# A fused encoder layer on one core: x and the small vectors laid out channel by channel, and the first two weight tiles taken slice by slice

## The chip, the cores and the metric

The kernel runs on one core of a Trainium2 chip. The metric is the device time of one execution in microseconds (us), as the median of several runs. A profiled execution of the same program gives the trace from which all rows below are taken.

## What is computed

One encoder layer on 256 tokens (a grid of 4 rows by 64 columns) with 2048 channels, all in float32. The part that matters here is the beginning:

```python
xn = rmsnorm(x, norm_pre_w)        # x (1, 256, 2048); scale by rsqrt(mean(x*x) + 1e-6), times norm_pre_w
h  = xn @ w_in                     # w_in (2048, 13312)
na_q, na_k, na_v, na_z, hg_q, hg_ff, hg_fb, hg_i, hg_z, gate_pre = split(h)
# o_a: neighbourhood attention on na_*, 16 heads of 64; o_b: gated two-way recurrence on hg_*, 8 heads of 128
g_a, g_b = split(sigmoid(gate_pre + b_gate))
y   = g_a * (o_a @ w_branch[:1024]) + g_b * (o_b @ w_branch[1024:])
out = x + rmsnorm(y @ w_out, norm_post_w)
```

## The kernel before

All products are made of rounded halves. A float32 operand is split into a high part (rounded to the matmul's format, ScalarE) and a low part (the remainder, VectorE), and a product is hi*hi + lo*hi + hi*lo, three matmuls. Weights come in tiles of 1 MiB into `raw`, a ring of four slots that SP's queue fills (`load`, line 318); a tile is split in two halves, by `split_hi` on ScalarE (line 463) and `split_lo` on VectorE (line 721), into `w_hi` and `w_lo`, four halves each.

The program has a beginning of 16 weight tiles (`early_tile`, line 1244), then 8 groups of ten tiles and 8 gate tiles (`project`, line 1174), then the branch and output products. The beginning is four blocks of 512 output columns (values of the attention, then inputs of the recurrence); a block is four tiles, and tile r of a block covers contraction slices k = 4r to 4r + 3. A slice is 128 channels. Each slice of an early tile is six matmuls of 128 x 512: three parts times two halves of the tokens.

Within the beginning, x has to be turned: it lies token by token in memory and the products want channels on partitions. x is loaded in token rows by six transfers on SP's queue (`load_x`, line 352), which lie between the weight slices of the first two tiles (`first_weights`, line 362). TensorE transposes each 128 x 128 square into PSUM (`turn_x`, line 1205); ScalarE reads the square out as the high part, times `norm_pre_w` (`first_hi`, `x_hi`, lines 564 and 570), VectorE makes the low part (`first_lo`, `x_lo`, lines 996 and 1005). The factor of the norm that belongs to a token is applied later. It comes from squares of x (`square`, line 575, ScalarE), a power on GpSimd (line 425) and a scaled identity (`make_turner`, line 1017), from which TensorE makes a row of factors for channel-major use (line 1255, ahead of the second half of tile 5). `take_block` (line 584) uses it for the blocks' results, `scale_pair`, `act_hi` and `act_lo` (lines 1024, 594 and 1034) for x itself, one pair of slices to a tile.

The small vectors (bounds, gate biases, two norm weights) are loaded as rows by four transfers on ScalarE's queue and are transposed on TensorE too (lines 1399 and 1403).

What sets the order is each engine's own program, written out by hand, with semaphores between them. Lines 366 to 383 are SP's order at the start: x and weight slices 0 to 7 by turns, then a wait for slices 4 to 7 (line 378), tile 2, a wait for the last x (line 381), tiles 3 to 15. TensorE warms up with six products of ones (line 1396), waits for the identity, transposes the norm weight, and goes through `first_tile` (line 1228). ScalarE squares x between the splits of tiles 1 and 2 and behind the last slice of x (lines 620 and 627).

Of the kernel before, what the change touches and what calls it, by code (L numbers as in the profile page):

```python
# [32 lines left out]
P = 128  # L33
T = 256
# [29 lines left out]
WARM_UP = 6  # L64
KEEP_WARM = 2
FIRST_K = 4
# [33 lines left out]
def encoder_layer(nc, x, norm_pre_w, w_in, b_gate, band_bias, hg_lb_logits, hg_norm_w, w_branch,  # L100
                  w_out, norm_post_w, out):
# [4 lines left out]
    with ExitStack() as ctx:  # L106
# [17 lines left out]
        o_tok = big[:, 16:32, :].rearrange("p (t a) c -> p t (a c)", t=2)  # L124
        bias = sb("bias", [P, 2, 2 * BAND])
# [19 lines left out]
        first_rows = bias[:, :, :].rearrange("p a k -> p (a k)")  # L145
        vec_rows, norm_rows = first_rows[0:72, 0:P], first_rows[0:KT, P:2 * P]
        vec = sb("vec", [P, 88])
# [24 lines left out]
        def dec_of(level):  # L172
# [7 lines left out]
        turn_bank = (None, *bank[1:4], bank[7], bank[0], bank[6], bank[1])  # L180
        first_turned = (bank[0], bank[6])
        ps_norm, ps_vec = bank[4][:, 0:KT], bank[7][:, 0:72]
# [9 lines left out]
        first_landed = [sem(f"first_landed{k}") for k in range(2 * FIRST_K)]  # L192
# [8 lines left out]
        vec_landed, norm_landed, norm_turned, norm_ready = (  # L201
            sem("vec_landed"), sem("norm_landed"), sem("norm_turned"), sem("norm_ready"))
        x_landed = [[sem(f"x_landed{side}{t}") for t in range(2)] for side in range(2)]
        x_first_landed = [sem(f"x_first_landed{t}") for t in range(2)]
# [3 lines left out]
        vec_turned, vec_ready = sem("vec_turned"), sem("vec_ready")  # L208
# [3 lines left out]
        xt_done, xhi_ready, xn_ready = sem("xt_done"), sem("xhi_ready"), sem("xn_ready")  # L212
# [33 lines left out]
        def grid_rows(ap, t):  # L246

            return ap[0].rearrange("(r u c) d -> u c r d", r=ROWS, u=2)[t]
# [68 lines left out]
        def _(sp):  # L317
# [34 lines left out]
            def load_x(first_k, last_k, t, landed):  # L352
                cols = slice(first_k * P, last_k * P)
                sp.dma_start(x_tok[:, t, cols], grid_rows(x, t)[:, :, cols]).then_inc(landed, 16)
# [14 lines left out]
            for k in range(2, FIRST_K):  # L369
                first_weights(k)  # L370
# [1127 lines left out]
```

## Time and profile before

| | us |
|---|---|
| median of 3 runs | 815.03 (813.36 to 815.8) |
| profiled execution | 813.89 |
| its span on the core | 812.2 |
| TensorE busy (matmuls) | 800.6 (99%) |
| VectorE busy | 626.2 (77%) |
| ScalarE busy | 391.2 (48%) |
| GpSimd busy | 25.4 (3%) |
| mean granted TensorE clock | 0.998 |

The page gives busy time as a share of the span. Matmuls are pipelined, so one of 128 x 512 lasts 0.39 us in the trace while the next starts 0.23 us after it; a busy TensorE is to be read by starts, not by durations. The trace has 13919 instructions, 5672 of them matmuls, and 153.52 MB of transfers.

### The profile page before, as it was taken

The numbers are of one execution on the slowest core, as the hardware profiler recorded it, in microseconds if no ns is written. First come the engines' busy times: TensorE is split into PE (matmuls) and PEld (weight loads), VectorE is DVE, ScalarE is ACT, GpSimd is POOL, SyncE is SP. The second block draws the span as 40 slices with busy tenths as digits, with TensorE's granted clock in tenths as the row PEclk, the third lists the DMA queues.
The fourth block names the chain that finished last, engine by engine and source line by source line (L and its number), as shares of the span: only waits on it lengthen the run. The fifth ranks groups of instructions, "written<-read, shape, count | busy, mean of one in ns | idle before, by whom it ended". The sixth has DMA issues, their size and how long they took to land.

```text
span 812.2 us, 13919 instructions
## 1 busy us (share of the span) xinstructions
PE 800.6 (99%) x5672; PEld 692.9 (85%) x5672; DVE 626.2 (77%) x1079; ACT 391.2 (48%) x668; POOL 25.4 (3%) x45
## 2 busy tenths in 40 slices
PE   9999999999999999999999999999999999999995
PEld 7788888888888888888888888888888888888884
DVE  4777647888888889889889889889874887865543
ACT  5755435445445444444544444445445555444442
POOL 4000000000000000000000000000000000000002
PEclk9999999999999999999999999999999999999999
DMA  8856578676676676666766756657667776586522
GB/s 306 307 172 212 155 193 229 172 203 172 164 207 166 174 198 165 187 184 170 195 171 182 193 161 195 185 157 197 167 168 197 209 203 178 187 297 219 187 73 104
DMA packets 238528, 153.52 MB, mean 189 GB/s; under 512 B 3752, under 2 KB 219904, under 8 KB 238080
## 3 DMA queue, kind: packets, MB, share of 16 engines
q1 hardware_dynamic: 237456, 148.65, 63.6%
q10 hardware_dynamic: 1008, 3.98, 1.3%
q8 instruction: 45, 0.74, 0.4%
q14 instruction: 19, 0.16, 0.1%
HBM read 149.47 MB, written 2.10 MB: 187 GB/s over the span
## 4 chain that ended last, share of the span: by engine, by line
PE 94%; DMA 1%; ACT 1%; SPq 1%; DVE 1%; POOL 0%; issue 0%; POOLq 0%; ACTq 0%
PE psum L1186 47%; PE psum L1194 25%; PE psum L1441 3%; PE psum L1443 3%; PE psum L1442 3%; PE psum L1270 3%; PE psum L1272 3%; PE psum L1271 3%; DMA raw<-in_w_in 1%; PE psum L1313 1%; PE psum L1347 1%; PE psum L1299 1%; PE psum L1336 1%; PE psum L1286 0%; SPq L363 0%
## 5 line engine op out<-in xcount | busy, mean ns | idle before, releaser
L725 DVE TENSOR_TENSOR w_lo<-raw,w_hi 128x1024 fp32r<-128x1024 f32 x270 | 320.2, 1221 | 70.6 <-ACT w_hi L471 70.5
L1186 PE MATMUL psum<-act_hl,w_hi 128*128 128x512 f32 x1408 | 335.8, 391 | 0.0
L471 ACT ACTIVATE w_hi<-raw 128x1024 fp32r<-128x1024 f32 x270 | 272.7, 1054 | 64.0 <-PE psum L1272 34.0
L1186 PEld LDWEIGHTS psum<-act_hl,w_hi 128*128 128x128 f32 x1408 | 258.8, 188 | 50.1
L1194 PE MATMUL psum<-act_hl,w_lo 128*128 128x256 f32 x1408 | 185.5, 285 | 0.0
L1194 PEld LDWEIGHTS psum<-act_hl,w_lo 128*128 128x128 f32 x1408 | 178.1, 191 | 4.8
L485 ACT ACTIVATE part<-psum 128x256 f32<-128x256 f32 x88 | 33.6, 382 | 227.2 <-PE psum L1194 227.2
L1186 PE MATMUL psum<-branch_hl,w_hi 128*128 128x512 f32 x256 | 61.4, 391 | 0.7 <-DVE branch_hl L925 0.7
L1186 PEld LDWEIGHTS psum<-branch_hl,w_hi 128*128 128x128 f32 x256 | 47.0, 188 | 10.2 <-issue 1.1
L1441 PE MATMUL psum<-w_hi,act_hl 128*128 128x512 f32 x128 | 49.9, 390 | 0.3 <-DVE w_lo L725 0.3
L1443 PE MATMUL psum<-w_hi,act_hl 128*128 128x512 f32 x128 | 49.8, 389 | 0.0
L1442 PE MATMUL psum<-w_lo,act_hl 128*128 128x512 f32 x128 | 49.8, 389 | 0.0
L1270 PE MATMUL psum<-w_hi,branch_hl 128*128 128x512 f32 x120 | 47.2, 393 | 0.9 <-DVE w_lo L725 0.6
L1272 PE MATMUL psum<-w_hi,branch_hl 128*128 128x512 f32 x120 | 46.7, 389 | 0.0
L1271 PE MATMUL psum<-w_lo,branch_hl 128*128 128x512 f32 x120 | 46.7, 389 | 0.0
L1194 PEld LDWEIGHTS psum<-branch_hl,w_lo 128*128 128x128 f32 x256 | 32.8, 191 | 1.2
L1194 PE MATMUL psum<-branch_hl,w_lo 128*128 128x256 f32 x256 | 33.2, 283 | 0.0
L742 DVE TENSOR_TENSOR hg<-psum,part 128x256 f32<-128x256 f32 x32 | 18.2, 568 | 16.4 <-ACT part L485 15.7
L783 DVE STREAM_TRANSPOSE prob_t<-wide 32x128 f32<-32x128 f32 (+1 forms) x96 | 27.9, 291 | 1.5
L1441 PEld LDWEIGHTS psum<-w_hi,act_hl 128*128 128x128 f32 x128 | 24.0, 188 | 5.6 <-DVE w_lo L725 0.8
L1443 PEld LDWEIGHTS psum<-w_hi,act_hl 128*128 128x128 f32 x128 | 24.0, 188 | 5.1
L1442 PEld LDWEIGHTS psum<-w_lo,act_hl 128*128 128x128 f32 x128 | 24.0, 188 | 5.0
(136 smaller groups left out, 616.7 us busy)
## 6 DMA issues: line engine op xcount, KB each, us to landing
raw<-in_w_in SPq DMA_DIRECT2D x102, 1024.0 KB, 5.8
raw<-in_w_branch SPq DMA_DIRECT2D x16, 1024.0 KB, 5.9
raw<-in_w_out SPq DMA_DIRECT2D x16, 1024.0 KB, 5.1
raw<-in_w_in SPq DMA_DIRECT2D x8, 256.0 KB, 5.6
big<-in_x ACTq DMA_DIRECT2D x2, 1024.0 KB, 6.4
bias<-in_band_bias SPq DMA_DIRECT2D x8, 192.0 KB, 5.9
out<-big SPq DMA_DIRECT2D x5, 256.0 KB, 2.6
big<-in_x SPq DMA_DIRECT2D x4, 256.0 KB, 4.9
```

The costliest lines, as they stand in the source:

```text
L471: nc.scalar.activation(w_hi[:, (2 * r + h) % HALVES, :], raw[:, r, 1024 * h:1024 * (h + 1)], ACT.Copy).then_inc(hi_ready, 1)
L485: nc.scalar.activation(part[:, b, :], ps_proj[b][:, T:2 * T], ACT.Copy).then_inc(part_ready, 1)
L725: nc.vector.tensor_tensor(w_lo[:, i, :], raw[:, r, 1024 * h:1024 * (h + 1)], w_hi[:, i, :].bitcast(F32), ALU.subtract).then_inc(lo_ready, 1)
L783: ins = nc.vector.transpose(*turned_square(r, j))
L1186: nc.tensor.matmul(sums[h][:, :], w_hi[:, i, w], operand[:, k, :], start=k == 0 if whole else k % 8 == 0, stop=False, skip_group_check=True)
L1194: ins = nc.tensor.matmul(sums[h][:, 0:T], w_lo[:, i, w], operand[:, k, 0:T], start=False, stop=k == KT - 1 if whole else k % 8 == 7, skip_ ...
L1270: nc.tensor.matmul(sums, hi, w_hi[:, i, w], start=(k == 0), stop=False)
L1271: nc.tensor.matmul(sums, hi, w_lo[:, i, w], start=False, stop=False)
L1272: ins = nc.tensor.matmul(sums, lo, w_hi[:, i, w], start=False, stop=(k == KT - 1))
L1441: nc.tensor.matmul(o, hi, w_hi[:, i, w], start=(k == 0), stop=False)
L1442: nc.tensor.matmul(o, hi, w_lo[:, i, w], start=False, stop=False)
L1443: ins = nc.tensor.matmul(o, lo, w_hi[:, i, w], start=False, stop=(k == KT - 1))
```

## The change

On the host, x is given twice: `x_turned`, channel by channel (128 partitions, 16 slices, 256 tokens), and `x_rows`, token by token in the kernel's own order of tokens; the vectors come as one array of 128 partitions by 88. The output is written in the kernel's order of tokens and is put back on the host.

In the kernel, transposes of x and of the vectors are gone, with the matmuls that kept TensorE warm between them. x is loaded in pairs of slices, the first pair and the vectors on ScalarE's queue, the others on SP's, between the weight slices; weight tiles 0 and 1 go slice by slice, slices 0 to 7, through `first_split_hi`, `first_split_lo` and `first_products`, and slice 0's high part is made by VectorE. SP waits for no landing at the start. Token-major x, needed for the squares, is loaded behind tiles 4 and 5; squares, power, scaled identity, gate constants, `take_block(0)` and the scaling of x move one or two tiles later. The warm-up has nine products.

The core of the diff:

```diff
-WARM_UP = 6
-KEEP_WARM = 2
-FIRST_K = 4
+WARM_UP = 9
+FIRST_K = 8
...
+        x_cols = big[:, 16:32, :]
...
         def store(engine, t, c):
-            engine.dma_start(grid_rows(out, t)[:, :, c * 512:(c + 1) * 512],
+            engine.dma_start(out[t * P:(t + 1) * P, c * 512:(c + 1) * 512],
...
# SP
+            def load_cols(i):
+                sp.dma_start(x_cols[:, 2 * i:2 * i + 2, :], x_turned[:, 2 * i:2 * i + 2, :]).then_inc(cols_landed[i], 16)
...
-            for t in range(2):
-                load_x(0, FIRST_K, t, x_first_landed[t])
-                first_weights(t)
-            for k in range(2, FIRST_K):
-                first_weights(k)
-            for t in range(2):
-                load_x(FIRST_K, 8, t, x_landed[0][t])
-            for k in range(FIRST_K, 2 * FIRST_K):
-                first_weights(k)
-            for t in range(2):
-                load_x(8, KT, t, x_landed[1][t])
-            for k in range(FIRST_K, 2 * FIRST_K):
-                sp.wait_ge(first_landed[k], 16)
-            early(2)
-            for t in range(2):
-                sp.wait_ge(x_landed[1][t], 16)
-            for n in range(3, N_PRE):
-                early(n)
+            for i in range(FIRST_K // 2):
+                if i:
+                    load_cols(i)
+                for k in (2 * i, 2 * i + 1):
+                    first_weights(k)
+            for n in range(2, 4):
+                for i in (2 * n, 2 * n + 1):
+                    load_cols(i)
+                early(n)
+            for n in range(4, N_PRE):
+                early(n)
+                if n < 6:
+                    t = n - 4
+                    sp.dma_start(x_tok[:, t, :], x_rows[t * P:(t + 1) * P, :]).then_inc(rows_landed[t], 16)
...
# ScalarE
             def x_hi(k):
-                act.wait_ge(xt_done, k // 2 + 2)
-                nc.scalar.activation(x_hl[:, k, 0:T], turn_bank[k // 2][:, (k % 2) * T:(k % 2 + 1) * T], ACT.Copy,
+                if k % 2 == 0:
+                    act.wait_ge(cols_landed[k // 2], 16)
+                nc.scalar.activation(x_hl[:, k, 0:T], x_cols[:, k, :], ACT.Copy,
                                      scale=norm_w[:, k:k + 1]).then_inc(xhi_ready, 1)
+            def square(t):
+                wait(act, ss_ready, 2 * t)
+                act.wait_ge(rows_landed[t], 16)
+                for side in range(2):
+                    nc.scalar.activation(squares[side], x_tok[:, t, side * (D // 2):(side + 1) * (D // 2)], ACT.Square,
                                          accum_out=ssq[:, 2 * side + t:2 * side + t + 1]).then_inc(ss_ready, 1)
...
+            act.dma_start(x_cols[:, 0:2, :], x_turned[:, 0:2, :]).then_inc(cols_landed[0], 16)
+            act.dma_start(vec[:, :], vectors).then_inc(vec_landed, 16)
+            act.wait_ge(const_step, 1)
+            nc.scalar.activation(small[:, 124:125], ones[:, 0:1], ACT.Copy)
+            act.wait_ge(vec_landed, 16)
+            for k in range(FIRST_K):
                 x_hi(k)
+                if k > 0:
+                    first_split_hi(k)
+            for n in range(2, 4):
+                for h in range(2):
+                    x_hi(4 * n + 2 * h)
+                    x_hi(4 * n + 2 * h + 1)
+                    split_hi(*early_place(n), h)
+            for n in range(3, N_PRE):
                 split_tile(*early_place(n + 1))
-                if n % 4 == 0:
+                if 4 <= n < 6:
+                    square(n - 4)
+                if n == 6:
+                    take_block(0)
+                elif n % 4 == 0 and n > 4:
                     take_block(n // 4 - 1)
...
-                if 7 <= n < 15:
-                    act_hi(n - 7)
+                if 8 <= n < 16:
+                    act_hi(n - 8)
...
# VectorE
+            dve.wait_ge(first_landed[0], 16)
+            nc.vector.tensor_copy(w_hi[:, 0, 0:512], raw[:, 0, 0:512]).then_inc(first_copied, 1)
+            dve.wait_ge(vec_landed, 16)
+            for i in range(KT // 2):
+                dve.wait_ge(cols_landed[i], 16)
+                if i < FIRST_K // 2:
+                    for k in (2 * i, 2 * i + 1):
+                        x_lo(k)
+                        first_split_lo(k)
+                else:
+                    x_lo(2 * i)
+                    x_lo(2 * i + 1)
+                    split_lo(i // 2, i // 2, i % 2)
+            for n in range(3, N_PRE):
                 split_tile(n + 1, (n + 1) % RAW)
...
+                if n == 5:
+                    rstd_set_up()
+                    gate_set_up()
+                if n == 6:
                     make_turner()
+                if n == 7:
                     dve.wait_ge(rows_ready, 1)
+                if 8 <= n < 16:
+                    act_lo(n - 8)
                 if 7 <= n < 15:
-                    act_lo(n - 7)
-                if 6 <= n < 14:
-                    scale_pair(n - 6)
+                    scale_pair(n - 7)
...
# TensorE
+            def first_products(k):
...
                 w = slice((k % 2) * 512, (k % 2 + 1) * 512)
+                def product(t, lo, weights, start=False):
+                    cols = slice(lo * T + t * P, lo * T + (t + 1) * P)
+                    return nc.tensor.matmul(bank[4 + t], x_hl[:, k, cols], weights[:, k // 2, w], start=start, stop=False)
+                pe.wait_ge(xhi_ready, k + 1)
+                if k == 0:
+                    pe.wait_ge(first_copied, 1)
+                else:
+                    pe.wait_ge(hi_ready if k % 2 else first_w_hi, k // 2 + k % 2)
+                for t in range(2):
+                    product(t, 0, w_hi, start=(k == 0))
+                pe.wait_ge(xn_ready, k + 1)
+                for t in range(2):
+                    product(t, 1, w_hi)
                 pe.wait_ge(lo_ready if k % 2 else first_w_lo, k // 2 + 1)
...
                 for t in range(2):
+                    ins = product(t, 0, w_lo)
+                if k % 2:
+                    ins.then_inc(half_used, 1)
...
-                    if (n, h) == (1, 1):
-                        pe.wait_ge(vec_ready, 1)
-                        for t in range(2):
-                            turn_x(8, KT, t, x_landed[1][t])
-                    if (n, h) == (5, 1):
+                    if (n, h) == (7, 0):
                         pe.wait_ge(turner_ready, 2)
...
             warm(WARM_UP)
+            for k in range(FIRST_K):
+                first_products(k)
             pe.wait_ge(const_step, 4)
-            pe.wait_ge(norm_landed, 16)
-            nc.tensor.transpose(ps_norm, norm_rows[:, :], block[0:KT, 0, 0:KT]).then_inc(norm_turned, 1)
-            warm(1)
-            first_tile()
-            pe.wait_ge(vec_landed, 3 * 16)
-            nc.tensor.transpose(ps_vec, vec_rows[:, :], block[0:72, 0, 0:72]).then_inc(vec_turned, 1)
-            for n in range(1, N_PRE):
+            for n in range(2, N_PRE):
                 early_tile(n)
```

## Rows read from the trace of the kernel before

**Rows 1.** The page, engines: busy us, share of the span, instructions.

```profile
PE 800.6 (99%) x5672; PEld 692.9 (85%) x5672; DVE 626.2 (77%) x1079; ACT 391.2 (48%) x668; POOL 25.4 (3%) x45
```

**Rows 2.** All waits of TensorE: for whom, us in total, times, longest.

```profile
PE psum L1215 <- POOL small L405: 1.1, 1, 1.1
PE psum L1186 <- DVE branch_hl L925: 0.7, 1, 0.7
...
PE psum L1441 <- DVE w_lo L725: 0.3, 1, 0.3
```

**Rows 3.** Timeline, TensorE: start us, us, line, tile, count, idle before and releaser.

```profile
28.71 0.47 PE L1270 MATMUL psum<-w_hi,branch_hl 128*128 128x512 f32 x1 [0.45 <-DVE w_lo L725]
...
42.21 0.39 PE L1272 MATMUL psum<-w_hi,branch_hl 128*128 128x512 f32 x1
```

**Rows 4.** Timeline, ScalarE ahead of tile 3.

```profile
25.16 1.10 ACT L581 ACTIVATE hg<-big 128x1024 f32<-128x1024 f32 x1
...
26.20 3.94 ACT L471 ACTIVATE w_hi<-raw 128x1024 fp32r<-128x1024 f32 x4
```

**Rows 5.** Timeline, ScalarE and VectorE on the first half of tile 2.

```profile
19.36 1.06 ACT L471 ACTIVATE w_hi<-raw 128x1024 fp32r<-128x1024 f32 x1 [2.12 <-DMA raw<-in_w_in]
20.46 1.23 DVE L725 TENSOR_TENSOR w_lo<-raw,w_hi 128x1024 fp32r<-128x1024 f32 x1 [3.90 <-ACT w_hi L471]
```

**Rows 6.** Transfers by line: issue ns, first and last issue us; landing times.

```profile
L354 SPq DMA_DIRECT2D big<-in_x x6: 546/586/716, 0.8 to 8.4; - x6
DMA to landing us min/median/max: 3.4/5.7/7.5
L363 SPq DMA_DIRECT2D raw<-in_w_in x8: 432/513/609, 1.5 to 7.3; - x8
DMA to landing us min/median/max: 3.4/5.6/6.1
L323 SPq DMA_DIRECT2D raw<-in_w_in x1: 394/394/394, 13.5 to 13.5; - x1
DMA to landing us min/median/max: 5.9/5.9/5.9
L323 SPq DMA_DIRECT2D raw<-in_w_in x1: 367/367/367, 23.6 to 23.6; - x1
DMA to landing us min/median/max: 6.9/6.9/6.9
```

**Rows 7.** Stretches: busy us by engine, granted clock, share of transfer engines, GB/s.

```profile
0.00:7.00 7.00, 5.94 (x26) 5.57 (x27) 0.81 (x3) 2.61 (x5) 6.09 (x15) 1.00 0.59 179
7.00:14.00 7.00, 6.56 (x34) 5.27 (x33) 5.28 (x11) 5.32 (x13) 3.19 (x9) 1.00 0.99 367
29.00:60.00 31.00, 31.00 (x140) 25.70 (x139) 22.26 (x41) 15.83 (x21) 1.61 (x1) 1.00 0.61 205
```

**Rows 8.** Timeline: weight loads of two runs of transposes, and the first product.

```profile
4.51 0.87 PEld L1209 LDWEIGHTS psum<-block,big 128*128 128x128 f32 x4
7.21 0.47 PE L1223 MATMUL psum<-w_hi,branch_hl 128*128 128x512 f32 x1
17.37 1.90 PEld L1209 LDWEIGHTS psum<-block,big 128*128 128x128 f32 x16
```

**Rows 9.** Timeline: splits of x and weights in the first tiles; the power.

```profile
5.97 0.63 ACT L560 ACTIVATE w_hi<-raw 128x512 fp32r<-128x512 f32 x1
8.21 0.84 ACT L572 ACTIVATE branch_hl<-psum,vec 128x256 fp32r<-128x256 f32 x2
9.10 0.48 DVE L1007 SCALAR_TENSOR_TENSOR branch_hl<-psum,vec,branch_hl 128x256 fp32r<-128x256 f32 x1
9.61 0.69 DVE L1042 TENSOR_TENSOR w_lo<-raw,w_hi 128x512 fp32r<-128x512 f32 x1
30.06 1.61 POOL L425 TENSOR_TENSOR small<-small 128x2 f32<-128x2 f32 x1 [19.66 <-DVE small L1015]
```

**Rows 10.** Remainders of the scaled x: durations, first and last start.

```profile
L1036 DVE TENSOR_TENSOR act_hl<-hg,act_hl x8: 683/684/693, 53.5 to 91.6; 128x512 fp32r<-128x512 f32 x8
```

More of the change, by code:

```diff
@@ L189, in encoder_layer @@
         x_pair = (hg[:, 0:2, :], hg[:, 2:4, :])
-        first_landed = [sem(f"first_landed{k}") for k in range(2 * FIRST_K)]
+        first_landed = [sem(f"first_landed{k}") for k in range(FIRST_K)]
+        first_copied = sem("first_copied")
         first_w_hi, first_w_lo = sem("first_w_hi"), sem("first_w_lo")
@@ L199, in encoder_layer @@
         tile_out = sem("tile_out")
[L201 to L204, printed above, removed]
+        vec_landed = sem("vec_landed")
+        cols_landed = [sem(f"cols_landed{i}") for i in range(KT // 2)]
+        rows_landed = [sem(f"rows_landed{t}") for t in range(2)]
         block_taken = sem("block_taken")
@@ L463, in split_hi @@
             def split_hi(n, r, landed, h):
-                if isinstance(n, int) and n == 1:
-                    for k in range(2):
-                        act.wait_ge(first_landed[FIRST_K + 2 * h + k], 16)
-                elif h == 0:
+                if h == 0:
                     act.wait_ge(raw_landed[r], landed)
@@ L1057, in _ @@
-            for h in range(2):
-                split_lo(2, 2, h)
-                x_lo(8 + 2 * h)
-                x_lo(9 + 2 * h)
-            for k in range(12, 16):
-                x_lo(k)
-            for n in range(2, N_PRE):
+            dve.wait_ge(first_landed[0], 16)
+            nc.vector.tensor_copy(w_hi[:, 0, 0:512], raw[:, 0, 0:512]).then_inc(first_copied, 1)
+            dve.wait_ge(vec_landed, 16)
+            for i in range(KT // 2):
[8 more added lines that the diff above has]
+                    split_lo(i // 2, i // 2, i % 2)
@@ L1196, in project @@
                     ins.then_inc(half_used, 1)
-            def turned(k, t):
-                if k < 2:
-                    return first_turned[t][:, k * P:(k + 1) * P]
-                c = (k % 2) * T + t * P
-                return turn_bank[k // 2][:, c:c + P]
-            def turn_x(first_k, last_k, t, landed):
-                pe.wait_ge(landed, 16)
-                for k in range(first_k, last_k):
-                    ins = nc.tensor.transpose(turned(k, t), x_tok[:, t, k * P:(k + 1) * P], block[:, 0, :])
-                    if k == 1 or (t == 1 and k % 2 == 1):
-                        ins.then_inc(xt_done, 1)
             def warm(count):
@@ L1247, in early_tile @@
                 for h in range(2):
-                    if (n, h) == (1, 1):
-                        pe.wait_ge(vec_ready, 1)
-                        for t in range(2):
-                            turn_x(8, KT, t, x_landed[1][t])
-                    if (n, h) == (5, 1):
+                    if (n, h) == (7, 0):
                         pe.wait_ge(turner_ready, 2)
```

151 lines of the change are left out of this document (31 added, 120 removed).

## The prediction

> **What bounds the kernel now.** I read the page first, then the list of waits, the timeline of the first 45 us, the transfers one by one, and the table of stretches. TensorE is busy for 99% of the span [rows 1]; the other engines have room. The list of waits says where TensorE loses what little it loses: six entries in 812 us, none over 1.1 us, and only two of them, 0.7 and 0.3 us, behind the first 30 us [rows 2]. So once its stream of matmuls is under way nothing moves the end except the number of matmuls and the moment from which the stream is unbroken. That moment is the first matmul of weight tile 3, at 28.71 us [rows 3]. From there 60 matmuls (tiles 3 and 4 and half of 5) begin over 13.50 us, one per 0.229 us [rows 3]; a tile has 24, so 5.49 us. Tiles 0 to 2 are 72 matmuls or 16.5 us. The other 12.2 of the first 28.7 us are start, transposes and stalls, and all the change can win lies there.
>
> Why is tile 3 not earlier? By the curve of landings below it was there at about 22 us, but ScalarE was copying and squaring until 26.2 us; only then come its split on ScalarE and its remainder on VectorE, on which TensorE waits the last 0.45 us [rows 3, 4]. Tile 2 shows the other limit: ScalarE waits 2.12 us for its landing, starts at 19.36, VectorE starts at 20.46 and ends at 21.69 [rows 5]: 2.33 us from landing to a usable half. Tile 2 landed late because SP held its issue until 13.47 us [rows 6].
>
> **The transfers set the pace after the change.** Issue plus the time to landing gives a curve of landed bytes. x's first quarter MiB lands at 0.8 + 3.4 = 4.2 us, the last weight slice (3.0 MiB in the queue's order) at 7.3 + 6.1 = 13.4, the last of x (4.0 MiB) at 8.4 + 7.5 = 15.9, tile 2 (5.0) at 13.5 + 5.9 = 19.4, tile 6 (9.0) at 23.6 + 6.9 = 30.5 [rows 6]. From 15.9 to 30.5 that is 2.92 us per MiB. The 16 engines are busy all the while (share 0.99 from 7 to 14 us) [rows 7], so another order of issues moves pieces along this curve and does not lift it.
>
> **Part by part.** *Removed.* All 32 transposes of x, the two of the vectors, the warming matmuls between them, and the PSUM copies of the vectors. The 16 transposes of the second half alone hold TensorE 1.90 us [rows 8]; the earlier ones are about 3 us more. None of this is subtracted again below: I sum along the new path.
>
> *The first two tiles.* x's first pair of slices goes on ScalarE's queue, weight slice 0 on SP's, both at about 0.8 us; half a MiB lands together by 4.9 us, where before the first x and weight pieces were both in (1.5 + 3.4) [rows 6]. The 45 KB of vectors follow the pair on ScalarE's queue. No row shows such a load of 128 short rows; the nearest are 1.7 us for a tiny one alone, and 3.4 us for a quarter MiB [rows 6], so 1.4 us of issue time plus these gives 3.1 to 4.8, and not before the pair ahead of it: I take 5.0. Everything on ScalarE (all copies and splits) is queued behind its new wait for the vectors; a late load shifts the start one for one. Then one copy of x, 0.42 us [rows 9]: first product at about 5.6, against 7.21 in the old trace. Nine warming matmuls, two passes each as slow as the first transposes (0.22 us) [rows 8], begin at 1.1 and end near 5.2, so they are not in the way.
>
> From there a slice needs a quarter MiB of weights and an eighth of x, 0.375 MiB, about 1.1 us of transfers; on ScalarE 0.42 + 0.63 us; on VectorE 0.48 + 0.69 us [rows 9]; on TensorE 6 × 0.229 = 1.37 us. TensorE is slowest, after a jerky beginning: the third slice waits for the sixth quarter MiB (about 8.4 us) plus 0.63, so 9.05; six slices more at 1.37 end at 17.3 us.
>
> *Tile 2* is what ends last. Ahead of it go 2 MiB of weights, 1.5 MiB of x and the vectors; with itself 4.54 MiB. On the curve: 15.9 + 0.54 × 2.92 = 17.5, or 17.8 by the steeper piece up to tile 2's own old landing; I take 17.65. Split, remainder and hand-over, 2.33 us plus about 0.1 for TensorE's start, give 20.05 us [rows 5]. ScalarE and VectorE are free by then (slice 7 lands by about 13.5 and is through at 15.7). TensorE therefore pauses from 17.3 to 20.05. The second half's splits end by about 22.2, inside the 2.75 us of the first. Tile 3 (6.04 MiB, 22.0 us) needs its split by 25.5 and has it near 24.6: squaring is no longer in ScalarE's queue there. So tile 3 begins at 20.05 + 5.49 = 25.5 us instead of 28.71: **3.2 us earlier**.
>
> *Token-major x behind tiles 4 and 5*, two 1 MiB transfers, moves past the loads of tiles 5 and 6 on SP's queue. Tile 6 is then 11.04 MiB: 30.5 + 2.04 × 2.92 = 36.5 us. TensorE reaches it at 25.5 + 3 × 5.49 = 42.0, so it must land by 39.6: 3 us to spare. From 29 to 60 us the engines carry 205 GB/s at a share of 0.61 [rows 7]; 2.1 MB more are 68 GB/s there. Squaring (four of 1.1 us with their sums [rows 4]) sits between the splits of tiles 5 to 7 on ScalarE; the power on GpSimd takes 1.61 us [rows 9]. My sum puts squares done at 40.5, the power at 42.5, the scaled identity at 46, against 47.5, where TensorE asks for it ahead of tile 7. Cover: 1.5 to 2 us, the thinnest here; beyond it a delay costs its own length. Scaling x runs one tile later: its last remainder began at 91.6 us [rows 10], and group 0 at 28.71 + 13 × 5.49 = 100.1, 8.5 later; a tile and the remainder itself, 5.49 + 0.68, go off that, and 2.3 us remain.
>
> *Priced at nothing:* output rows stored straight and the tail's x read straight (same bytes, pieces of 2 KB or more), the dummy copy that pulls ScalarE's table load forward, the moved gate constants.
>
> **Sum.** The profiled execution took 813.89 us (span 812.2); less 3.2 it is 810.7. It lies 1.1 under the median of 815.03; against the median the forecast is **811.8 us**. Tile 2 landing at 17.2 (the 2.5 us per MiB between 13.4 and 15.9) or at 18.5 (vectors slow, queues sharing) makes the gain 3.6 or 2.3.
>
> **Rivals.** *1. The clock falls in the new pause.* The granted clock reads 1.00 (2.4 GHz) in every stretch [rows 7], but the same weight loads of transposes take 218 ns apiece at 4.5 us and 119 at 17.4 [rows 8], near the ratio of the levels 2.4 and 1.2 GHz: the engine began at the lower one, after standing idle, and rose by about 7 us: the first product, at 7.21, lasts 0.47 us like the one at 28.71 [rows 3, 8]. If 2.75 us of standing brings it down, tile 2 begins at the lower level; a half tile there costs 12 × 0.229 = 2.75 us more, about what the 5.9 slow us of the start cost (2.95). Gain 0.4, time 814.6. For it: behind the start no wait of the old list is over 0.7 us [rows 2]. Against: the stop ahead of tile 3 did no harm, and TensorE may run later into the pause and shorten it. A clock that is merely slow to rise during slices 0 to 7 costs nothing up to 2.75 us, since the pause takes it up. 18%. The Trainium skill ("TensorE: Matmul & The Clock Gate", "Why this matters for your kernels") warns of dropping the clock by idling between bursts; by that rule this rival is the one to fear, and the old trace has no pause long enough to show it.
>
> *2. Slower: the rows of x hold up the weights.* If reads of x's rows drag the transfers so that tile 6 lands after 39.6 us, each us late costs one. From 42.8 the gain is gone; at 45.3 the kernel is 2.5 us slower, 817.5. That needs 11.04 MiB at under 275 GB/s, where the stretch from 7 to 14 us shows 367 [rows 7]. The squares' chain ends in the same wait. 7%.
>
> *3. Transfers better than the curve.* By the table of stretches 1.25 MB have moved by 7 us and 367 GB/s follow [rows 7]; the 4.76 MB up to tile 2's end are through at 16.6 us, and if no engine trails the others tile 2 lands near 16.9: gain 3.9 or a little more, time 811.0. 9%.
>
> *4. It does not do what it says:* vectors or the first slices land so late that all slips by 2 us or more, 813.5 to 815. 6%.
>
> **How the numbers follow.** My forecast holds 60%; it covers gains of 2.3 to 3.9. A measurement can tell about 0.3% or 2.4 us. Faster by more than that: nearly all of the forecast (0.55) and rival 3 (0.09), 0.64; within it: the rest, rivals 1 and 4 and a mild 2, 0.29; slower 0.07. The range, 810.5 to 814.7, takes in tile 2's bounds and rivals 1 and 3.
>
> **What would show it.** Right: first product near 5.6, slice 7 done near 17, one pause of 2 to 3.5 us ahead of tile 2, released by VectorE behind a landing near 17.6; tile 3 at 25.5; no further TensorE waits but the two known ones. Wrong: matmuls 0.43 us apart behind the pause (rival 1); a wait at tile 6 or 7 (rival 2); a first product after 7 us (rival 4).

## The result, and the profile after

| | before | after |
|---|---|---|
| median | 814.51 us (813.36 to 815.8, 4 runs) | 809.59 us (809.46 to 809.67, 4 runs) |
| profiled execution | 813.89 us | 809.55 us |
| its span | 812.2 us | 807.8 us |

The ratio is 0.994, with a 95% interval of 0.9928 to 0.9952: a small gain, but clear of the noise, 4.9 us in the medians and 4.3 us between the profiled executions. The forecast was 811.8, with a range down to 810.5; the time is 0.9 us below the range. The sign and most of the path were right, the size was not.

The page after the change, engines; then all waits of TensorE:

```profile
PE 795.5 (98%) x5638; PEld 688.9 (85%) x5638; DVE 626.7 (78%) x1080; ACT 391.5 (48%) x666; POOL 25.3 (3%) x45
...
PE psum L1200 <- DVE w_lo L688: 1.5, 1, 1.5
PE psum L1152 <- POOL small L390: 1.1, 1, 1.1
PE psum L1160 <- ACT branch_hl L549: 1.0, 1, 1.0
PE psum L1138 <- DVE branch_hl L888: 0.7, 1, 0.7
```

TensorE is about as full as before [rows 1]. Two waits are new: 1.5 us for the remainder of a weight tile, and 1.0 us ahead of the first product, for the first copy of x. Gone are the short waits of the first 30 us (0.6, 0.4 and 0.3 us in total by line) and the 0.3 us in the output product (L1441 before, [rows 2]).

The timeline of TensorE after, which answers to [rows 3, 8]: warm-up, first product, the last pair of slice 7, the first matmuls of tiles 2 and 3.

```profile
1.05 4.21 PE L1152 MATMUL psum<-ones 128*128 128x128 f32 x18 [1.05 <-POOL small L390]
6.28 1.35 PE L1160 MATMUL psum<-w_hi,branch_hl 128*128 128x512 f32 x4 [1.01 <-ACT branch_hl L549]
...
17.27 0.61 PE L1160 MATMUL psum<-w_lo,branch_hl 128*128 128x512 f32 x2
19.35 0.47 PE L1200 MATMUL psum<-w_hi,branch_hl 128*128 128x512 f32 x1 [1.47 <-DVE w_lo L688]
...
24.88 0.39 PE L1200 MATMUL psum<-w_hi,branch_hl 128*128 128x512 f32 x1
```

Tile 3 begins at 24.88 instead of 28.71: 3.83 us earlier. The last matmul begins at 799.37 instead of 803.65, 4.28 earlier, and the span is 4.4 shorter. So 3.8 of the 4.4 us come from the beginning and about half a us from the end of the kernel.

ScalarE and VectorE on the first copy of x and the first half of tile 2 (answering to [rows 5]), and SP's issues of the first two weight slices, of tile 2 and of the first rows of x (with [rows 6]):

```profile
5.71 0.91 ACT L549 ACTIVATE branch_hl<-big,vec 128x256 fp32r<-128x256 f32 x2 [2.49 <-DMA vec<-in_vectors]
16.89 1.06 ACT L453 ACTIVATE w_hi<-raw 128x1024 fp32r<-128x1024 f32 x1 [2.39 <-DMA raw<-in_w_in]
17.98 1.23 DVE L688 TENSOR_TENSOR w_lo<-raw,w_hi 128x1024 fp32r<-128x1024 f32 x1 [2.23 <-ACT w_hi L453]
...
0.80 0.86 SPq L352 DMA_DIRECT2D raw<-in_w_in  x2
7.18 0.58 SPq L313 DMA_DIRECT2D raw<-in_w_in  x1
12.38 2.47 SPq L368 DMA_DIRECT2D big<-in_x_rows  x1
```

Tile 2 is issued at 7.18 (before at 13.47), has landed when ScalarE starts at 16.89 (before at 19.36), and reaches TensorE 2.5 us later, by the same two steps as before.

Stretches after, columns as in [rows 7]:

```profile
0.00:7.00 7.00, 4.93 (x21) 4.32 (x21) 1.12 (x3) 2.77 (x5) 6.09 (x14) 1.00 0.71 231
7.00:14.00 7.00, 7.00 (x31) 5.50 (x31) 7.00 (x14) 6.31 (x14) 3.92 (x10) 1.00 1.05 376
19.40:24.00 4.60, 4.60 (x21) 3.81 (x22) 4.47 (x9) 4.13 (x8) 0.00 (x0) 1.00 1.06 409
```

In the first 7 us the transfers now carry 231 GB/s at a share of 0.71, against 179 at 0.59 in [rows 7]; in the next 7 us, 376 against 367. In both kernels little moves in the first 2 us (at most 25 GB/s), which lowers both shares; from 3 to 7 us it is 366 GB/s at a share of 1.04 after, 285 at 0.89 before.

The other half us is at the start of the output product, in ScalarE's program: first the place before the change, then the same place after it (ACTq is ScalarE's queue, which issues the tail's x; L471 and L453 split the first output weights right behind).

```profile
718.36 1.29 ACTq L680 DMA_DIRECT2D big<-in_x  x2
719.75 3.90 ACT L471 ACTIVATE w_hi<-raw 128x1024 fp32r<-128x1024 f32 x4 [0.98 <-PE psum L1443]
722.13 0.50 PE L1441 MATMUL psum<-w_hi,act_hl 128*128 128x512 f32 x1 [0.35 <-DVE w_lo L725]
```

```profile
714.57 0.82 ACTq L643 DMA_DIRECT2D big<-in_x_rows  x2
715.49 3.91 ACT L453 ACTIVATE w_hi<-raw 128x1024 fp32r<-128x1024 f32 x4 [0.51 <-PE psum L1369]
```

Two issues in the split pattern take 1.29 us of ScalarE, two plain ones 0.82. Before, the splits behind them came too late: one step between two matmuls was 0.74 us instead of 0.23. After the change the longest step there is 0.34 us.

### The profile page after: what moved, and what is told of

It is laid out like the page before. It is cut to its first block, busy times and chain, and to the rows that moved or that the text cites. A ratio compares the mean times of both kernels' runs of the same rounds, so it can differ in the third digit from the quotient of the medians.

```text
span 807.8 us, 13847 instructions
## 1 busy us (share of the span) xinstructions
PE 795.5 (98%) x5638; PEld 688.9 (85%) x5638; DVE 626.7 (78%) x1080; ACT 391.5 (48%) x666; POOL 25.3 (3%) x45
## 4 chain that ended last, share of the span: by engine, by line
PE 96%; DMA 1%; SPq 1%; POOL 0%; ACT 0%; DVE 0%; issue 0%; POOLq 0%; ACTq 0%
PE psum L1138 47%; PE psum L1146 25%; PE psum L1367 3%; PE psum L1369 3%; PE psum L1368 3%; PE psum L1200 3%; PE psum L1201 3%; PE psum L1202 3%; PE psum L1243 1%; DMA raw<-in_w_in 1%; PE psum L1277 1%; PE psum L1229 1%; PE psum L1266 1%; PE psum L1216 0%; SPq L352 0%; POOL big L437 0%
## 5 line engine op out<-in xcount | busy, mean ns | idle before, releaser
L453 ACT ACTIVATE w_hi<-raw 128x1024 fp32r<-128x1024 f32 x268 | 270.7, 1053 | 61.3 <-PE psum L1202 27.6
L1200 PE MATMUL psum<-w_hi,branch_hl 128*128 128x512 f32 x112 | 43.8, 391 | 1.5 <-DVE w_lo L688 1.5
L1201 PE MATMUL psum<-w_lo,branch_hl 128*128 128x512 f32 x112 | 43.6, 389 | 0.0
L1202 PE MATMUL psum<-w_hi,branch_hl 128*128 128x512 f32 x112 | 43.6, 389 | 0.0
```

Of the source, the lines that this page charges most:

```text
L453: nc.scalar.activation(w_hi[:, (2 * r + h) % HALVES, :], raw[:, r, 1024 * h:1024 * (h + 1)], ACT.Copy).then_inc(hi_ready, 1)
L1200: nc.tensor.matmul(sums, hi, w_hi[:, i, w], start=(k == 0), stop=False)
L1201: nc.tensor.matmul(sums, hi, w_lo[:, i, w], start=False, stop=False)
L1202: ins = nc.tensor.matmul(sums, lo, w_hi[:, i, w], start=False, stop=(k == KT - 1))
```

## The experiments

Theory: what is won is tile 2's landing, and the landing came earlier than forecast because the start on two queues saves issue time; the pause ahead of tile 2 is the price left over. Rivals: the order alone (no holds, squares later) did it; the pause costs the clock; the tail's x does more than half a us. Each kernel is the changed one with the edit shown, unless it says "before". The changed kernel was timed in one session only, four runs, and the others in other sessions, between which the median of the kernel before moved from 814.08 to 814.75 us. Differences of a few tenths of a us between medians are therefore not shown by the medians alone; the readings rest on the traces.

**The order alone**, in the kernel before: SP's holds go, and squares, power, identity and scaling move as in the change; x is still turned on TensorE.

```diff
-            for k in range(FIRST_K, 2 * FIRST_K):
-                sp.wait_ge(first_landed[k], 16)
-            early(2)
-            for t in range(2):
-                sp.wait_ge(x_landed[1][t], 16)
-            for n in range(3, N_PRE):
+            for n in range(2, N_PRE):
                 early(n)
...
-            square(0)
...
-            square(1)
...
+                if 4 <= n < 6:
+                    square(n - 4)
```

> The kernel before with only the order changed: SP's two holds gone, and squares, power, scaled identity, gate constants and the scaling of x one or two tiles later, as in the change; x is still turned on TensorE. Theory (the holds and squaring gave tile 3 its late start, but the transposes fill TensorE): tile 2 without its stop, at 22.1 us, tile 3 at 27.5 instead of 28.7: 1.2 us faster than before. Rival (order alone carries the whole gain): 4 us faster. Rival (layout alone carries it): no change.

Measured: 812.85 us (812.59 to 813.87, 11 runs), ratio 0.9984 (0.9975 to 0.9992): 1.2 us faster than before in the same session, as expected. The first split of tile 2, and the first matmul of tile 3:

```profile
19.22 1.06 ACT L466 ACTIVATE w_hi<-raw 128x1024 fp32r<-128x1024 f32 x1 [3.72 <-DMA raw<-in_w_in]
...
27.95 0.39 PE L1267 MATMUL psum<-w_hi,branch_hl 128*128 128x512 f32 x1
```

The first matmul of tile 2 in the kernel before, for comparison:

```profile
22.52 0.50 PE L1270 MATMUL psum<-w_hi,branch_hl 128*128 128x512 f32 x1 [0.26 <-DVE branch_hl L1007]
```

Tile 2 is issued at 9.2 instead of 13.5 and yet lands at 19.2, as before [rows 5]. So lifting SP's hold is worth nothing to tile 2's landing there; tile 3 comes to 27.95 us because ScalarE no longer squares in front of its split. Of the 4.9 us this order explains 1.2. For the rest the transposes have to go: tile 2 begins at 22.45 here, as in the kernel before (22.52), since TensorE is busy until then with transposes and tiles 0 and 1. This is not the whole of the change's order, though. Half a MiB of x still lies ahead of tile 2 that the change puts behind it; what that alone is worth was not run.

**SP's holds back**, in the changed kernel:

```diff
-            for n in range(2, 4):
-                for i in (2 * n, 2 * n + 1):
-                    load_cols(i)
-                early(n)
+            for i in range(4, 8):
+                load_cols(i)
+            for k in range(4, FIRST_K):
+                sp.wait_ge(first_landed[k], 16)
+            early(2)
+            for i in range(6, 8):
+                sp.wait_ge(cols_landed[i], 16)
+            early(3)
```

> The changed kernel with SP's two old holds put back: tile 2 is issued only when weight slices 4 to 7 have landed, tile 3 only when the last pair of x has. Theory (it is SP's order that brought tile 2 forward): issue near 13, landing near 19, tile 2's products at 21.4, tile 3 at 26.9: 2.0 us slower, 811.6. Rival (the earlier landing comes from x's layout and the two queues, not from the holds): within 0.4 us of 809.6.

Measured: 810.96 us (810.23 to 813.28, 6 runs), ratio 0.9959 (0.9944 to 0.9975), 1.4 us slower than the change, where 2.0 were expected. SP's issues of the last four pairs of x and of tiles 2 to 4, ScalarE's first split of tile 2, and TensorE's wait:

```profile
6.47 2.46 SPq L343 DMA_DIRECT2D big<-in_x_turned  x4
12.87 3.55 SPq L313 DMA_DIRECT2D raw<-in_w_in  x3
...
18.26 1.06 ACT L457 ACTIVATE w_hi<-raw 128x1024 fp32r<-128x1024 f32 x1 [3.78 <-DMA raw<-in_w_in]
...
PE psum L1204 <- DVE w_lo L692: 2.6, 1, 2.6
```

Landing, tile 2 (20.72) and tile 3 (26.25) all slip by the same 1.37 us, and so does the median: from tile 2's landing to the end nothing absorbs a delay. What made the landing late is not settled by this run, since the edit does two things. It holds tile 2's issue, and it puts two more pairs of x, half a MiB, ahead of it, which at the 2.5 to 2.9 us per MiB of the forecast's curve would by themselves be 1.25 to 1.45 us (an estimate).

**One queue for all**: the first pair of x and the vectors go on SP's queue, ahead of weight slice 0.

```diff
 # ScalarE
-            act.dma_start(x_cols[:, 0:2, :], x_turned[:, 0:2, :]).then_inc(cols_landed[0], 16)
-            act.dma_start(vec[:, :], vectors).then_inc(vec_landed, 16)
 # SP
+            load_cols(0)
+            sp.dma_start(vec[:, :], vectors).then_inc(vec_landed, 16)
             for i in range(FIRST_K // 2):
                 if i:
                     load_cols(i)
```

> The changed kernel with the first pair of x slices and the vectors on SP's queue ahead of weight slice 0, nothing on ScalarE's queue at the start. In the changed kernel 231 GB/s moved in the first 7 us against 179 before, and tile 2 landed at 16.9 us, 0.8 ahead of the old curve. Theory (two queues that start at once lift the curve): 190 GB/s or less in the first 7 us, tile 2 lands at 17.5 or later. Rival (x's plain layout does it, by shorter issues and even pieces): 220 to 231 GB/s and tile 2 within 0.4 us of 16.9. The time stays within 0.8 us of 809.6 either way.

Measured: 811.92 us in one run, 2.4 us over the changed kernel's profiled execution; the expectation that the time would stay within 0.8 us failed. SP's first issues, the first split of tile 2, TensorE from there, and the first 7 us with the columns of [rows 7]:

```profile
0.80 0.39 SPq L343 DMA_DIRECT2D big<-in_x_turned  x1
1.25 0.42 SPq L356 DMA_DIRECT2D vec<-in_vectors  x1
1.72 0.90 SPq L352 DMA_DIRECT2D raw<-in_w_in  x2
...
17.73 1.06 ACT L455 ACTIVATE w_hi<-raw 128x1024 fp32r<-128x1024 f32 x1 [2.38 <-DMA raw<-in_w_in]
...
20.19 0.47 PE L1200 MATMUL psum<-w_hi,branch_hl 128*128 128x512 f32 x1 [2.54 <-DVE w_lo L688]
...
20.96 0.57 PE L1200 MATMUL psum<-w_hi,branch_hl 128*128 128x512 f32 x1
21.33 0.63 PE L1201 MATMUL psum<-w_lo,branch_hl 128*128 128x512 f32 x1
...
24.60 0.39 PE L1200 MATMUL psum<-w_hi,branch_hl 128*128 128x512 f32 x1
...
0.00:7.00 7.00, 4.85 (x23) 4.14 (x23) 1.84 (x4) 2.39 (x4) 6.09 (x14) 1.00 0.69 189
```

Two things are to be seen. The first is the start. Weight slice 0 is issued 0.92 us later (0.80 to 1.72), which is the issue time of the two loads put ahead of it, and tile 2 lands 0.84 us later (16.89 to 17.73). That the two numbers nearly agree is in part chance: in the three other executions with the change's order on SP, tile 2 landed at 16.58, 16.27 and 16.21 (the kernels with one warming product, the tail's old pattern and the vectors first, below), so that one queue costs 0.84 to 1.5 us. The rate says the same on more executions. In the first 7 us the eight profiled kernels that start on two queues carry 221 to 243 GB/s, the eight executions with the old start 175 to 208, and this one, with the new layout on one queue, 189. So it is the second queue that lifts the start and not the layout of x, as far as one execution on one queue can tell, and this is what the forecast lacked. The Trainium skill ("Trainium Kernel Development and Optimization", "Key Constraints") states that issuing from several engines only saves the sequencer's issue time; the trace agrees in size, with 0.84 to 1.5 us at the landing for 0.92 us of issue time.

The second thing is the pause: by its landing (17.7, forecast 17.65) and its end (20.2, forecast 20.05) it is the one that was forecast, and behind it matmuls start 0.43 us apart (21.33 to 24.32) with a granted clock of 0.50, the lower level. Tile 2 lasts 7.16 us instead of 5.53; 0.84 + 1.63 = 2.47 at tile 3. In this one execution rival 1 comes true.

**Rows of x ahead of tile 2**, the strong form of that pause:

```diff
+            for t in range(2):
+                sp.dma_start(x_tok[:, t, :], x_rows[t * P:(t + 1) * P, :]).then_inc(rows_landed[t], 16)
             for n in range(2, 4):
...
-                if n < 6:
-                    t = n - 4
-                    sp.dma_start(x_tok[:, t, :], x_rows[t * P:(t + 1) * P, :]).then_inc(rows_landed[t], 16)
```

> The changed kernel with the two 1 MiB loads of token-major x moved from behind tiles 4 and 5 to ahead of tile 2. Theory (tile 2's landing sets the start of tile 3, one for one): 2 MiB at about 2.65 us each put it 5.3 us later, tile 3 near 30.2, 814.9, with matmuls 0.23 us apart behind a pause of about 7 us. Rival (a pause of that length brings TensorE's clock down): matmuls about 0.43 us apart at first, 2 to 3 us more, 817 to 818.

Measured: 817.12 us (816.05 to 817.55, 8 runs), ratio 1.0032 (1.0022 to 1.0042): slower than before, as the rival said. TensorE from slice 7 on:

```profile
18.84 0.61 PE L1159 MATMUL psum<-w_lo,branch_hl 128*128 128x512 f32 x2
24.63 0.76 PE L1199 MATMUL psum<-w_hi,branch_hl 128*128 128x512 f32 x1 [5.17 <-DVE w_lo L687]
25.19 0.63 PE L1200 MATMUL psum<-w_lo,branch_hl 128*128 128x512 f32 x1
...
27.32 0.47 PE L1199 MATMUL psum<-w_hi,branch_hl 128*128 128x512 f32 x1
...
31.49 0.39 PE L1199 MATMUL psum<-w_hi,branch_hl 128*128 128x512 f32 x1
```

Tile 2 begins 5.28 us later than in the changed kernel, and six slow matmuls (24.63 to 27.32, 2.69 us instead of 1.36) add 1.33: tile 3 is 6.61 later, the profiled execution 6.56. Against the place ahead of tile 2, putting token-major x behind tiles 4 and 5 is thus worth more than the whole change.

**Two half tiles**: tiles 2 and 3 are loaded in pieces of half a MiB, each behind the pair of x slices that it needs.

```diff
-                for i in (2 * n, 2 * n + 1):
-                    load_cols(i)
-                early(n)
+                for h in range(2):
+                    load_cols(2 * n + h)
+                    sp.dma_start(raw[:, n, 1024 * h:1024 * (h + 1)].rearrange("p (k c) -> p k c", k=2),
+                                 w_in_v[:, 4 * n + 2 * h:4 * n + 2 * h + 2, V_TILE * P:V_TILE * P + 512]
+                                 ).then_inc(raw_landed[n] if h else half_landed[n - 2], 16)
```

> The changed kernel with weight tiles 2 and 3 loaded as two half MiB pieces each, a pair of x slices ahead of each piece, so that a half can be split as soon as it has landed. Theory (the pause of 1.5 us ahead of tile 2 is its landing at 16.9 us plus 2.4 us of split, and nothing else): the first half lands near 15, is split by 17.4, TensorE goes on from the first tiles at 17.7 without a pause, tile 3 starts at 23.2 instead of 24.9: 1.6 us faster, 808.0. Rival (the engines' transfers are the bound and a finer cut moves nothing): tile 3 within 0.3 us of 24.9, 809.6.

Measured: 809.37 us (807.9 to 809.83, 6 runs), ratio 0.9934 (0.9922 to 0.9947), where 808.0 was expected. First the split of the first half of tile 2, then a stretch of the slices, with the columns of [rows 7]:

```profile
14.95 1.06 ACT L458 ACTIVATE w_hi<-raw 128x1024 fp32r<-128x1024 f32 x1 [0.36 <-DMA raw<-in_w_in]
...
6.30:9.70 3.40, 3.37 (x8) 2.69 (x9) 3.29 (x6) 2.86 (x7) 3.19 (x7) 1.00 1.02 345
```

The half lands nearly 2 us earlier and the pause is gone, but little of it reaches the end. In this execution TensorE was slow at the start: eight matmuls in 3.4 us, 0.43 us apart. The slices ended at 18.9 and tile 3 began at 24.37, 0.5 earlier than in the change. A slow start that the pause had hidden was now the bound; the best of the six runs, 807.9, is as short as those of the next kernel.

**The same with twelve warming products** instead of nine:

```diff
-WARM_UP = 9
+WARM_UP = 12
```

> The changed kernel with tiles 2 and 3 in half MiB pieces and twelve warming products instead of nine, so that TensorE has no gap between the last of them and the first product at 6.3 us. In the run with pieces alone the slices ran 0.43 us apart until 9.8 us, ended at 18.9 and hid the gain; one of its six executions took 807.9. Theory (the rise of the clock, late by the gap in the warm-up, ate it): matmuls 0.23 us apart from about 7 us, slices end by 17.8, tile 3 at 23.2 to 23.5, 808.0 to 808.3. Rival (the moment of the rise doesn't hang on the gap): a spread from 807.9 to 809.9 as before.

Measured: 808.03 us (807.8 to 808.21, 6 runs), ratio 0.9919 (0.9906 to 0.9933): the fastest here, 1.6 us under the change. All waits of TensorE, and its first matmul of tile 2:

```profile
PE psum L1157 <- POOL small L393: 1.1, 1, 1.1
PE psum L1165 <- ACT branch_hl L554: 0.9, 1, 0.9
PE psum L1143 <- DVE branch_hl L893: 0.7, 1, 0.7
...
17.80 0.39 PE L1205 MATMUL psum<-w_hi,branch_hl 128*128 128x512 f32 x1
```

TensorE goes from slice 7 into tile 2 without a stop, and tile 3 begins at 23.24, 1.6 us earlier than in the change. The gap that the edit was to close is still there, though: TensorE waits 0.9 us ahead of the first product instead of 1.1. That all six runs are near the best one of nine products is shown; why three more products keep the start fast is not shown, and twelve products without the half tiles were not run.

**One warming product** in the changed kernel (`WARM_UP = 1`):

> The changed kernel with one warming product instead of nine. Theory (the pause ahead of tile 2 takes up whatever the slices lose): the clock rises later, slices 0 to 7 run some matmuls 0.43 us apart, the pause shrinks from 1.5 us, the time is 809.6 unless more than 1.5 us are lost. Rival (the warm-up carries part of the gain): 1 to 3 us slower.

Measured: 810.08 us (809.8 to 810.33, 5 runs), ratio 0.9944 (0.9931 to 0.9958). TensorE's second slice:

```profile
8.79 1.91 PE L1160 MATMUL psum<-w_hi,branch_hl 128*128 128x512 f32 x4
10.49 1.05 PE L1160 MATMUL psum<-w_lo,branch_hl 128*128 128x512 f32 x2
```

Two slices went at 0.43 us a matmul until 11.35. Tile 3 began at 25.04, only 0.16 later, the span is 0.3 longer and the median 0.5 up: the pause took up the slow start nearly whole, as the forecast said. (Tile 2 landed at 16.58 here, and no wait ahead of it was left.)

**Vectors ahead of the first pair of x** on ScalarE's queue (the two issues change places):

> The changed kernel with the vectors ahead of the first pair of x slices on ScalarE's queue. The first product waits for the vectors until 5.7 us; they should land near 4 us here and the pair near 5, so the first product comes 0.3 to 0.6 us earlier. Theory (tile 2's landing ends last): 809.6, tile 3 still at 24.9, the pause longer by what the start gains. Rival (the start sets the end): 0.3 to 0.6 us faster.

Measured: 809.49 us (809.03 to 810.01, 5 runs), ratio 0.9937 (0.9924 to 0.9949).

```profile
5.75 0.91 ACT L549 ACTIVATE branch_hl<-big,vec 128x256 fp32r<-128x256 f32 x2 [2.52 <-DMA big<-in_x_turned]
...
16.21 1.06 ACT L453 ACTIVATE w_hi<-raw 128x1024 fp32r<-128x1024 f32 x1 [2.39 <-DMA raw<-in_w_in]
```

ScalarE now waits for the pair instead of the vectors, and starts at the same time. Whichever of the two is second ends at 5.7 us, so this run didn't give the earlier start that was to be tested. What it does show is the spread: tile 2 landed 0.68 us earlier than in the changed kernel's own profile, but the first slices ran 0.43 us apart, and tile 3 began only 0.26 us earlier, at 24.62.

**The tail's x in the old pattern**, the output stored as in the change:

```diff
-                act.dma_start(x_tok[:, t, :], x_rows[t * P:(t + 1) * P, :]).then_inc(tail_landed, 16)
+                act.dma_start(x_tok[:, t, :], x[0].rearrange("(r u c) d -> u c r d", r=ROWS, u=2)[t]).then_inc(tail_landed, 16)
```

> The changed kernel with x at the tail loaded as before, in the old order of tokens (each half gathered as 32 columns by 4 rows), everything else unchanged. Theory (the old pattern costs ScalarE 0.24 us more of issue time for each of two transfers, and the first split of the output product waits behind them): issue of the two takes 1.3 instead of 0.8 us and TensorE waits about 0.5 us at the second output tile: 810.1. Rival (the 0.5 us wait in the old trace was chance or transfers in each other's way): 809.6, no wait there.

Measured: 809.92 us (809.82 to 810.45, 5 runs), ratio 0.9944 (0.9932 to 0.9957).

```profile
714.46 1.26 ACTq L643 DMA_DIRECT2D big<-in_x  x2
715.83 3.90 ACT L453 ACTIVATE w_hi<-raw 128x1024 fp32r<-128x1024 f32 x4 [0.95 <-PE psum L1369]
...
718.20 0.50 PE L1367 MATMUL psum<-w_hi,act_hl 128*128 128x512 f32 x1 [0.31 <-DVE w_lo L688]
```

The long issue, the late split and the wait of TensorE are back together, with a step of 0.70 us between two matmuls. The median is 0.33 us up, and in the trace the last matmul begins 0.34 us later (799.71 against 799.37): the step's 0.47 us (0.70 less 0.23), less the 0.1 us by which this execution reached the output product sooner.

**The kernel before, six more profiled executions**, to learn why its timed runs spread over 813.2 to 817.1 us (the changed kernel's four lie within 0.2 us). Two theories stood: the clock rises late at the start, or it falls a second time.

> The kernel before, unchanged, profiled once more. Its 17 timed runs of one session spread from 813.2 to 816.5 us, while those of the changed kernel lie within 0.3 us. Theory (the clock rises at another moment in each execution, and before has no pause that takes it up): in a run over 814.5 the first products are 0.43 us apart beyond 8 us and all stops behind them come later; in a run near 813.5 the clock is up by 7.3. Rival (the spread arises elsewhere): first products alike, and tile 3 at 28.7 in either.

> The kernel before once more, for a second execution with another moment of the clock's rise; same expectations as for the first repeat: time above 814.5 with a rise beyond 8 us, near 813.5 with one by 7.3 us, or, by the rival, no connection.

> The kernel before, unchanged. Its timed runs gather near 813.5, 815.1 and 816.5 to 817.1 us; three profiled ones (813.89, 814.20, 814.01) begin tile 3 at 28.7, 28.8 and 28.6 us, though the clock rose at 7.2, 10.4 and 4.8: a late rise alone isn't the spread. Theory (in the slower executions the clock falls once or twice again within the first 28 us, where transposes and stops leave TensorE little to do): an execution at 815 shows one stretch at a granted clock of 0.50 behind the first rise, about 1.7 us lost, one at 816.5 or more shows two. Rival (the loss lies behind 28 us, in transfers): tile 3 at 28.7 whatever the time.

> As for the third repeat of the kernel before: a time near 813.5 to 814.2 with tile 3 at 28.6 to 28.9, or 815 with one stretch at a granted clock of 0.50 ahead of tile 3 and tile 3 1.7 us later; by the rival, tile 3 at 28.7 whatever the time.

> As for the third repeat of the kernel before: a time near 813.5 to 814.2 with tile 3 at 28.6 to 28.9, or 815 with one stretch at a granted clock of 0.50 ahead of tile 3 and tile 3 1.7 us later; by the rival, tile 3 at 28.7 whatever the time.

> As for the third repeat of the kernel before: a time near 813.5 to 814.2 with tile 3 at 28.6 to 28.9, or 815 with one stretch at a granted clock of 0.50 ahead of tile 3 and tile 3 1.7 us later; by the rival, tile 3 at 28.7 whatever the time.

Measured: 814.20, 814.01, 814.75, 813.91, 813.21 and 813.89 us. Tile 3's first matmul in the fastest of them, then in the slowest:

```profile
28.03 0.47 PE L1270 MATMUL psum<-w_hi,branch_hl 128*128 128x512 f32 x1 [0.36 <-DVE w_lo L725]
```

```profile
29.18 0.47 PE L1270 MATMUL psum<-w_hi,branch_hl 128*128 128x512 f32 x1 [0.44 <-DVE w_lo L725]
```

Tile 3 begins at 28.03 in the fastest and 29.18 in the slowest: 1.15 of the 1.54 us between them. Three others lie between in both (28.6 to 28.8 us, 813.9 to 814.2); the last, 813.89, began tile 3 at 28.24 and lost half a us somewhere behind it. In one the clock rose late (matmuls 0.43 us apart until 10.4) and still it took 814.20; in none did it fall again. So within 813 to 815 us the time mostly follows the start of tile 3, and the theory of the second fall has nothing for it. Runs of 815 to 817 us occurred among the timed ones, but none was caught in a profile: why those are longer stays open. The two longest, 816.53 and 817.12, read a mean granted clock of 0.995, all others of this kernel 0.996 to 0.998, so a fall of the clock is possible in those two and not shown.

## Why the prediction was off, point by point

*Right.* That nearly all hangs on tile 3's first matmul (3.83 of the 4.28 us at the last one), and that a delay of tile 2's landing goes one for one to the end (holds back: 1.37 us at the landing and in the median). The slices' end, 17.7 against 17.3. The 2.33 us from landing to a usable half, plus 0.1 (16.89 to 19.35 is 2.46). One pause ahead of tile 2, released by VectorE behind a landing, though of 1.5 us and not 2.75. No wait at tiles 6 and 7: tile 6 landed at about 34.4 (forecast 36.5), squares were done at 39.1 (40.5), the scaled identity at 44.4 (46), so the cover named the thinnest was thicker. A slow rise of the clock costs almost nothing within the pause (one warming product: tile 3 0.16 us later).

*The step that failed* is the sentence "another order of issues moves pieces along this curve and does not lift it". It was right for an order: with the order alone tile 2 lands at 19.2 as before. But the change also starts a second queue, and that lifts the curve from its start: 221 to 243 GB/s in the first 7 us on two queues, 189 on one with the same layout, 175 to 208 with the old start. The row was there to be read: a share of 0.59 in the first 7 us [rows 7] says that the transfer engines were not full then, and "busy all the while" holds only from 7 us on. Part of that low share is the first 2 us, in which little moves before or after; the rest is 0.89 against 1.04 from 3 to 7 us. The 52 GB/s more in the first 7 us are 0.36 MB, or 0.35 MiB; at 2.5 to 2.9 us per MiB that is 0.9 to 1.0 us, and tile 2 landed 0.8 us ahead of the forecast (16.89 against 17.65). So tile 3 came 3.83 us earlier, not 3.2. A reading next to it was wrong too, without harm to the sum: "Tile 2 landed late because SP held its issue until 13.47 us". With the hold gone it is issued at 9.2 and lands no sooner (the order alone).

*A term priced at nothing was worth half a us.* The tail's x "read straight" was costed by its transfers, which are hidden. Its two issues stand in ScalarE's program ahead of the first split of the output weights, and there was no cover behind that split. Long issues are shown to bring the wait back (tail's x in the old pattern); 0.33 us in the medians, 0.47 in the trace.

*The offset.* The sum was made against the profiled 813.89 and carried its 1.14 us below the median of 815.03 along. After the change profile and median differ by 0.04 us. The offset belonged to the spread of the kernel before, whose other sessions had medians of 814.08 to 814.75, and should not have been carried. The three parts, 0.6 + 0.5 + 1.1, are the 2.2 us between 811.8 and 809.59, and the offset is the largest of them. Without it the forecast of 810.7 would have missed by 1.1.

*Smaller misses.* The first product was at 6.28, not 5.6, since the vectors were taken as landed at 5.0 and came at 5.7; the pause took that up.

*Rivals.* Rival 3 gave the landing (16.9) and the gain (3.9) that came, for another reason: it took 1.25 MB as moved by 7 us, and 1.62 MB had moved. It also took every byte by 16.9 us as one that tile 2 needs, while the 318 GB/s up to then are 5.37 MB, 0.6 more than the 4.76: later loads moved beside it. The two misses cancelled, which is luck. Rival 1 didn't come in the change, but its mechanism is real. The Trainium skill ("TensorE: Matmul & The Clock Gate", "Why this matters for your kernels") warns against idle gaps between bursts; the trace agrees behind the waits of 2.5 us (one queue) and 5.2 us (rows of x ahead), while behind 2.6 us with SP's holds and 1.5 us in the change the matmuls stayed 0.23 us apart. In these traces the length of a wait alone does not say whether the clock falls. Its price was over-estimated: 1.63 and 1.33 us, not 2.75, since only nine and six matmuls were slow. Of the two profiled executions with a wait of about the forecast length one lost the clock, so 18% looks low for the pause that was forecast, as far as two can tell. One of the unprofiled runs with SP's holds, 813.28 us at a mean clock of 0.995 where the others took 810.2 to 811.0 at 0.997 or 0.998, may be another. In the change the landing came earlier and the pause was shorter. Rival 2's mechanism is real too: put ahead of tile 2, the rows of x moved it 5.28 us back, while behind tiles 4 and 5 they held nothing up.

## What to carry to other kernels

Before a landing curve is used for a new order, look at the busy share of the transfer engines at each point of it: where they are not full, an earlier issue, here from a second queue, shifts everything behind. Count an issue as an instruction of the engine that issues it, above all where that engine's next instruction feeds a full TensorE. When a pause is taken away (half tiles), ask what it was hiding; here it was the slow start of TensorE's clock: with half tiles alone one of six runs gained 1.6 us, with twelve warming products as well all six did.

## What the runs showed of the hardware that was not expected

The granted clock reads 1.00 in the stretch from 6.3 to 9.7 us of the kernel with half tiles, while its matmuls start 0.43 us apart; ahead of the first rise the spacing tells the level and that column does not. In the kernel with the tail's x in the old pattern the granted clock was 0.50 from 7.5 to 10.8 us, behind the same nine warming products after which the changed kernel's matmuls were 0.23 us apart from 8.2 us on: the same start came out at either level. There the clock had risen within the warming (18 passes in 3.70 us instead of 4.21) and fell again behind a wait of 1.6 us.

A load of 1 MiB issued from SP in the queue's busy beginning takes long to land: tile 2 took 9.7 us from its issue and the rows of x 13.8 and 16.2, where one weight tile takes 5.8 in the median, at about 376 to 409 GB/s in all.
